# Modulation weights in pieces of 256 rows by 2048 columns, the first shift and scale rows turned on TensorE: a two-layer backbone step on one Trainium2 core

## The reference

```python
def modulation(cond, w, b):                      # w: (1024, 6144)
    m = jnp.einsum('bd,de->be', jax.nn.silu(cond), w) + b
    return [t[:, None, :] for t in jnp.split(m, N_MOD, axis=-1)]   # 6 rows of 1024

shift1, scale1, gate1, shift2, scale2, gate2 = mods
h = rms_norm(x, lw['norm1']) * (1 + scale1) + shift1
z = jnp.einsum('bsd,de->bse', h, lw['w_in'])     # projections q, kv, qr, kr, vr, ...
...                                              # attention, retention, gated MLP
x = x + gate1 * jnp.einsum('bsd,de->bse', mix, lw['w_out'])
h2 = (rms_norm(x, lw['norm2']) * (1 + scale2) + shift2)
...                                              # router, 16 experts
x = x + gate2 * y
```

## Time and profile before

| | |
|---|---|
| median of three runs | 2380.5 us |
| the profiled execution | 2377.39 us, span 2375.6 us |
| PE busy | 2141.1 us, 90% of the span |
| DVE busy | 1230.3 us, 52% |
| ACT busy | 818.0 us, 34% |
| Pool busy | 266.3 us, 11% |
| mean of granted TensorE clock | 0.948 of full speed |
| moved by DMA | 417.13 MB, mean 176 GB/s |

### The profile page before, as it was taken

The page is one execution under the profiler, slowest core; times in us unless marked ns, Lnnn a source line. Parts: engine busy times, 40 slices in busy tenths (PEclk is TensorE's granted clock), DMA queues, the critical chain, the costliest instruction groups (busy, mean ns, idle before and its releaser), DMA issues.

```text
span 2375.6 us, 25634 instructions
## 1 busy us (share of the span) xinstructions
PE 2141.1 (90%) x10487; PEld 1604.0 (68%) x10487; DVE 1230.3 (52%) x1630; ACT 818.0 (34%) x1030; POOL 266.3 (11%) x222
## 2 busy tenths in 40 slices
PE   1899989999999969999849999999999996799992
PEld 0587555488886448888627855647888844688881
DVE  0386455322222448888655844532232234788883
ACT  1123533100000127887532155221000011587881
POOL 2133020100000021000031411001000000110002
PEclk9899989999999959999969999999999996799996
DMA  7226440221134269999551337011121133699984
GB/s 264 107 71 226 149 151 1 74 87 71 36 107 160 99 235 370 415 409 412 212 217 36 109 116 240 10 71 54 62 81 72 40 146 142 226 414 415 411 356 151
DMA packets 113912, 417.13 MB, mean 176 GB/s; under 512 B 7801, under 2 KB 9961, under 8 KB 89089
## 3 DMA queue, kind: packets, MB, share of 16 engines
q1 hardware_dynamic: 89088, 329.27, 36.5%
q0 software_dynamic: 19920, 68.31, 7.6%
q10 hardware_dynamic: 4784, 17.87, 1.8%
HBM read 378.89 MB, written 36.54 MB: 175 GB/s over the span
## 4 chain that ended last, share of the span: by engine, by line
PE 88%; DVE 5%; DMA 3%; ACT 1%; issue 1%; SPq 0%; PEldq 0%; POOL 0%; DVEq 0%; ACTq 0%; POOLq 0%
PE ps L655 76%; PE ps L773 3%; PE ps L785 2%; PE ps L666 2%; PE ps L1039 1%; DMA ring_lo<-in_w_mod_dram 1%; PE ps L1050 1%; DMA work<-y_dram,slots_u 1%; DVE work L1627 1%; PE ps L774 1%; DVE work L1902 1%; DVE work L1904 1%; DVE work L1905 1%; SPq L448 0%; DMA work<-h_dram,slots_u 0%
## 5 line engine op out<-in xcount | busy, mean ns | idle before, releaser
L1859 DVE TENSOR_TENSOR expert_low<-ring_lo,expert_high 128x2048 fp32r<-128x2048 f32 x172 | 386.2, 2285 | 2.9 <-ACT expert_high L1392 2.9
L1392 ACT ACTIVATE expert_high<-ring_lo 128x2048 fp32r<-128x2048 f32 x172 | 326.3, 1914 | 108.0 <-PE ps L655 88.4
L655 PE MATMUL ps<-ring_lo,hT 128*128 128x512 f32 (+1 forms) x800 | 315.8, 552 | 12.5 <-ACT hT L1206 12.3
L655 PEld LDWEIGHTS ps<-ring_lo,hT 128*128 128x128 f32 x800 | 150.3, 191 | 160.3 <-issue 156.6
L655 PE MATMUL ps<-expert_high,x_high 128*128 128x512 f32 x512 | 207.6, 405 | 9.6 <-DVE expert_low L1859 9.6
L655 PE MATMUL ps<-branch,ring_lo 128*128 128x320 f32 x768 | 214.4, 432 | 0.0
L655 PE MATMUL ps<-expert_high,x_low 128*128 128x512 f32 x512 | 202.2, 395 | 0.0
L1341 ACT ACTIVATE work<-ps 128x640 f32<-128x640 f32 x48 | 33.8, 704 | 485.5 <-PE ps L655 485.4
L655 PE MATMUL ps<-expert_low,x_high 128*128 128x512 f32 x512 | 200.9, 392 | 0.0
L655 PE MATMUL ps<-h_hi,w_hi 128*128 128x320 f32 x768 | 186.2, 324 | 2.6 <-issue 2.6
L655 PEld LDWEIGHTS ps<-branch,ring_lo 128*128 128x128 f32 x768 | 143.5, 190 | 53.3
(11 more groups left out here) (272 smaller groups left out, 3283.4 us busy)
## 6 DMA issues: line engine op xcount, KB each, us to landing
ring_lo<-in_w_up_dram SPq DMA_DIRECT2D x64, 1024.0 KB, 7.9
ring_lo<-in_w_gate_dram SPq DMA_DIRECT2D x54, 1024.0 KB, 7.6
ring_lo<-in_w_down_dram SPq DMA_DIRECT2D x54, 1024.0 KB, 8.1
ring_lo<-in_w_in_dram SPq DMA_DIRECT2D x26, 2048.0 KB, 8.3
ring_lo<-in_w_mod_dram SPq DMA_DIRECT2D x24, 2048.0 KB, 13.6
y_dram<-branch ACTq DMA_DIRECT2D x32, 512.0 KB, 8.3
work<-in_w_down_dram SPq DMA_DIRECT2D x10, 1024.0 KB, 7.9
work<-in_w_gate_dram SPq DMA_DIRECT2D x10, 1024.0 KB, 8.4
```

The source lines that it names most:

```text
L655: return pe.matmul(out, lhsT, rhs, start=(k == 0), stop=(k == n - 1))
L1392: A(e_high[n % HIGH], e_raw[n % RAW], ACT.Copy).then_inc(ec_a.sem, 1)
L1859: TT(out=e_low[n % RAW], in0=e_raw[n % RAW], in1=e_high[n % HIGH].bitcast(F32), op=ALU.subtract).then_inc(el_v.sem, 1)
```

## The change

- **Pieces.** A piece of a group is now 256 rows by all 2048 columns of the group (runs of 8 KB in DRAM), two blocks k. `mod_group` waits for piece k // 2 only when it comes to it.
- **Their own signal.** The last matmul of each piece signals a new semaphore, `mod_pc`; SP waits on that for the piece's slot.
- **Turned on PE.** The rows of group 0, copied by ACT to partitions 32j and 32j+1 of a 128 x 512 area that Pool has set to zero, are transposed whole, with four PE transposes into PSUM bank 6, and DVE picks the 32 columns with one strided copy. Norm1's 8 rows are transposed by themselves and copied with a second DVE instruction. The four stores and two loads of group 0 through `mod_dram` and the waits for them are gone, in both layers.
- **Inputs in two parts.** norm1 and w_spatial (`first_inputs`) are loaded first; the other 12 DMAs (`layer_inputs`) are issued, in layer 0, once piece 2 has landed. PE's wait for them is now after the projections q and kv.

```diff
     def last_read(key):
         if key[0] == "mod":
-            return mod_mm, NGRP * key[1] + key[2] // 4 + 1
+            return mod_pc, MODT * key[1] + key[2] + 1
...
     def source(key):
         if key[0] == "mod":
-            return rows(I["w_mod"][key[1], :, key[2] * 512:(key[2] + 1) * 512]), KD, 512
+            g, j = divmod(key[2], 4)
+            return rows(I["w_mod"][key[1], 2 * P * j:2 * P * (j + 1), 2048 * g:2048 * (g + 1)]), 2, 2048
...
     def mod_group(l, g, b):
         pe.wait_ge(bias_in[g], 16 * (l + 1))
-        for j in range(4):
-            key = ("mod", l, 4 * g + j)
-            pe.wait_ge(full[slot_of[key]], full_at(key))
         for k in range(KD):
+            key = ("mod", l, 4 * g + k // 2)
+            if k % 2 == 0:
+                pe.wait_ge(full[slot_of[key]], full_at(key))
+            wt = slot[slot_of[key]]
             for j in range(4):
-                wt = slot[slot_of["mod", l, 4 * g + j]]
-                pe.matmul(ps[32 * j:32 * j + 2, b, :], scT[:, k:16:KD], wt[:, k * 512:(k + 1) * 512],
-                          start=(k == 0), stop=False)
+                c = 2048 * (k % 2) + 512 * j
+                i = pe.matmul(ps[32 * j:32 * j + 2, b, :], scT[:, k:16:KD], wt[:, c:c + 512],
+                              start=(k == 0), stop=False)
+            if k % 2 == 1:
+                i.then_inc(mod_pc, 1)
...
         pe.wait_ge(mod_ev, MODT * l + 4)
-        w(pe, aux_in, l, aux_in.per)
-        w(pe, modr_in, l, 32)
-        pe.transpose(ps[:, 4, 0:40], mod_rows, ident[0:40, 0:40]).then_inc(au_p.sem, 1)
+        w(pe, au_in, l, 32)
+        pe.transpose(ps[:, 4, 0:KD], norm_rows, ident[0:KD, 0:KD])
+        for c in range(4):
+            i = pe.transpose(ps[:, 6, c * P:(c + 1) * P], mod_area(l, 0)[1][:, c * P:(c + 1) * P], ident)
+        i.then_inc(au_p.sem, 1)
...
+        w(pe, aux_in, l, aux_in.per)
         for s, name in enumerate(("qr", "kr")):
...
     # ACT, start of a layer
-        act.wait_ge(mod_st, 64 * (NGRP * l + 1))
         modulate(0)
...
     # DVE, start of a layer
-        V.tensor_copy(modc, bank(4, 40)).then_inc(mc_v.sem, 1)
+        step.mark(V.tensor_copy(modc[:, 32:40], bank(4, KD)))
+        V.tensor_copy(modc[:, 0:32].rearrange("p (s j c) -> p s j c", s=2, j=4),
+                      bank(6).rearrange("p (c j r) -> p r j c", c=4, j=4)[:, 0:2]).then_inc(mc_v.sem, 1)
+        step.settle()
...
     # Pool, start of the program
+    G.memset(mod_area(0, 0)[1], 0.0).then_inc(zeroed, 1)
+    G.wait_ge(zeroed, 1)
     load_bias(0, 0)
...
+    first_inputs(0)
+    G.wait_ge(full[slot_of["mod", 0, 2]], full_at(("mod", 0, 2)))
     layer_inputs(0)
-    store_mods(0, 0)
-    G.wait_ge(mod_st, 64)
-    first_mod_rows(0)
...
     # Pool, end of layer 0
+    G.memset(mod_area(l + 1, 0)[1], 0.0).then_inc(zeroed, 1)
+    G.wait_ge(zeroed, l + 3)
     load_bias(l + 1, 0)
     w(G, lo_p, l, 1)
+    first_inputs(l + 1)
     layer_inputs(l + 1)
...
     fetch_rows(0)
-    store_mods(l + 1, 0)
-    G.wait_ge(mod_st, 64 * (NGRP * (l + 1) + 1))
-    first_mod_rows(l + 1)
```

More of the change, by code:

```diff
@@ L223, in trunk @@
         ws_raw = aux[:, 768:1280]
-        mod_rows = aux[0:40, 1280:1408]
+        norm_rows = aux[0:8, 1280:1408]
         kc_raw = aux[:, 1408:1536]
@@ L234, in trunk @@
         mod_mm = sem("mod_mm")
+        mod_pc = sem("mod_piece_read")
         mod_ev = sem("mod_ev")
@@ L278, in trunk @@
         full = [sem(f"slot{s}_full") for s in range(6)]
-        aux_in = signal("aux_in", 16 * 14)
-        modr_in = signal("mod_rows_in", 32)
+        au_in = signal("norm_and_spatial_in", 32)
+        aux_in = signal("aux_in", 16 * 12)
         xs_out = signal("xs_out", 16)
@@ L1933, in spread, with first_inputs @@
                 return G.dma_start(out, ap.partition_broadcast(P))
+            def first_inputs(l):
+                G.dma_start(norm_rows, I["norm1"][l].rearrange("(k p) -> k p", p=P)).then_inc(au_in.sem, 16)
+                G.dma_start(ws_raw.rearrange("p (g j) -> p g j", g=4),
+                            I["w_spatial"][l].rearrange("g i j -> i g j")).then_inc(au_in.sem, 16)
             def layer_inputs(l):
-                G.dma_start(mod_rows[32:40, :], I["norm1"][l].rearrange("(k p) -> k p", p=P)).then_inc(aux_in.sem, 16)
                 for out, nm in ((qk_gain[:, 0:DH], "q_norm"), (qk_gain[:, DH:2 * DH], "k_norm"),
@@ L1941, in layer_inputs @@
                     spread(out, I[nm][l]).then_inc(aux_in.sem, 16)
-                G.dma_start(ws_raw.rearrange("p (g j) -> p g j", g=4),
-                            I["w_spatial"][l].rearrange("g i j -> i g j")).then_inc(aux_in.sem, 16)
                 with nc.allow_non_contiguous_dma(reason="512 numbers, once per layer"):
@@ L2004, in _ @@
                     G.memset(zeros, 0.0).then_inc(zeroed, 1)
-                    G.wait_ge(zeroed, 1)
+                    G.wait_ge(zeroed, 2)
                     for half in range(2):
@@ L2035, in _ @@
                 w(G, xs_out, l, 16)
-                G.wait_ge(mod_st, 64 * NGRP * (l + 1))
+                G.wait_ge(mod_st, 128 * (l + 1))
                 w(G, cm_v, l, NT)
@@ L2077, in _ @@
                 fetch_rows(0)
-                if l + 1 < LAYERS:
-                    store_mods(l + 1, 0)
-                    G.wait_ge(mod_st, 64 * (NGRP * (l + 1) + 1))
-                    first_mod_rows(l + 1)
                 for e in range(1, NE):
```

## The result

The changed kernel takes 2361.7 us in the median of five runs (2359.9 to 2368.0), the kernel before, timed beside it, 2379.2 (2376.4 to 2380.7): a ratio of 0.9936, with a 95% interval of 0.9918 to 0.9954. It is 15.2 us faster by that ratio. The profiled execution took 2361.74 us around a span of 2359.9, against 2377.39 and 2375.6 before, 15.7 less. The forecast was 24.0 less. The time lies inside the range, by its upper end.

A forecast was written before the change was run, and what follows sets the result against it. TensorE bounds nearly the whole span, standing still at the start for modulation weights and rows. Terms -23.5 - 1.0 + 0.2 + 0.3 = -24.0 us took 2377.4 to 2353.4; forecast 2354 us, range 2347 to 2362.

The forecast's parts named there:

- forecast 35.0: Start of layer 0: the last piece of group 0's modulation weights lands at 35.0 us, where before it was 42.9.
- forecast 3.4 and 2.5: Start: after its landing piece 3's 16 matmuls take 3.4 us at the lower clock, ACT's copy of the rows 2.5.
- the step on q's weights: First projection: q's weights follow piece 3 and land at 45.5 to 48.5 us, in time for 48.8; no PE wait.
- I take even shares: DMA engines at the start: two busy queues were taken to share evenly, judged from bytes moved; called the weak point.
- rival B: First projection: q's weights come late behind inputs and x store; projection at 53 us, total 2358 us; chance 0.08.
- the forecast start: The first projection starts at 48.8 us instead of 72.27, 23.5 us earlier.
- rival A: Last piece held up by inputs, or 8 KB runs bring nothing: landing 40.2 to 42.9, total 2359 to 2362 us; chance 0.14.
- three signs of being wrong: Last piece landing after 40 us, PE waiting for q's weights, or later stages giving time back.
- the forecast's later terms: After the start: -1.0 us at layer 0's gather of h, +0.2 for four waits, +0.3 at layer 1's start.
- The 2.0: Start: held-back inputs, about 0.6 MB in flight beside piece 3, delay its landing by 2 us.
- The 33: Start: without the held-back inputs the last piece would land at 33 us, 32.0 at 425 GB/s.
- rival C: SP's queue takes more with 8 KB packets: pieces by 30.5, x at 31.5, projection at 48.6 us; chance 0.09.

The follow-up runs named there:

- e3: Changed kernel, but both the 12 layer inputs and the store of x are issued only once q's weights have landed; median 2354.6 us, ratio 0.9901.
- e1: Changed kernel, but the store of x is issued only once q's weights have landed; median 2356.0 us, ratio 0.9908.
- e2: Changed kernel, but the 12 layer inputs wait for q's weights while the store of x goes early; one run, 2358.3 us.
- e5: Changed kernel, but group 0's shift and scale rows go through DRAM again in both layers; median 2365.2 us, ratio 0.9941.
- e11: e3 plus ten unread filler matmuls, 1, 2 and 5 behind pieces 0, 1 and 2, two during ACT's row copy; median 2349.9 us, ratio 0.9878.
- e12: e11 with three filler matmuls behind piece 2 instead of five; median 2349.7 us, ratio 0.9878.
- e4: Changed kernel, but the store of x goes in four transfers of 256 columns, with runs of 1 KB; one run, 2362.0 us.
- e6: Changed kernel, but the 12 layer inputs are issued at the start as before, not after piece 2; median 2360.2 us, ratio 0.9922.
- e10: Changed kernel, but x is loaded in eight transfers of 256 columns, with runs of 1 KB; one run, 2365.8 us.
- e8: The changed kernel again, unaltered, as common measure beside e5 to e7; median 2361.4 us, ratio 0.9931.
- e7: Changed kernel, but with the old pieces of 512 columns (runs of 2 KB) and the group's signal; median 2370.1 us, ratio 0.9962.
- e9: Changed kernel, but SP waits for the group's last matmul, not each piece's own, before reloading the slots; median 2369.7 us, ratio 0.9962.

## Why the prediction was right in part

**Right: the place and most of the road.** PE stood still at the start for weights and rows, the change took both waits away, and from the second projection to the last expert's matmuls the lead grew by no more than 0.5 us. Piece 3 came at 34.3 (forecast 35.0), its burst cost 3.4 and the rows' copy 2.4 (forecast 3.4 and 2.5). In e3, where nothing stands in q's way, the bias took 1.9 as forecast, and from the first transpose to the projection it is 5.6 (forecast 6.0): the projection starts at 47.8. That its span is 24.1 us shorter, against 24.0 forecast, is in part luck: 24.5 at the start, 2.0 more on the way, 2.4 lost at the end.

**Wrong: the step on q's weights, which put PE's wait for them at nothing.** It said "At half the bandwidth q lands at about 45.5; at a third, at 48.5. Needed: 48.8." They landed at 51.8, and PE waited 6.3 us. Two things in it failed. The first is the rate. From piece 3's landing at 34.3 until then the engines moved some 6.0 MB, of which q was 2.1, a third, as allowed for (254, then 383, 411 and 400 GB/s); but 2.1 MB at a third in the 13.5 us from 35.0 means 470 GB/s, which no row of before reached, while 35 to 40 us ran at 254 GB/s with the small ones. At the 400 GB/s that its half was reckoned with, a third lands at 50.7, already 1.9 us late. The second is "I take even shares". Even was the number of packets, not of bytes: q's are half as large as the store's, so it had a third. The trace of before had this to show. From 10 to 15 us x's queue moved 1.37 MB and the weights' 0.65; piece 0 and x came out about even because piece 0 had started first. The same holds of the weights of "qr" and the store of x, where they ran side by side (from 70 to 72 us 136 packets against 129, 0.28 MB against 0.53).

This was rival B, given 0.08, and e1 to e3 show it: take either companion away and the wait is gone. The cost against the forecast start is 3.1 us. The time measured is also the price of rival A, 2359 to 2362, but not by its road: piece 3 was not late. That the time lies in the range is thus no merit of the sum. Of the three signs of being wrong that the prediction named, two came: PE waits for q's weights, and the end gives time back.

**Not priced: what the wait does to the clock.** Rival B gave 2358 for a start at 53. The wait itself also left PE at 1.2 GHz for about the first 6 us of the projection: 13.53 us instead of 10.56, another 3.0. The Trainium skill, "TensorE: Matmul & The Clock Gate", section "HAM oscillation — how this bites in real kernels", warns of waits for transfers between bursts of matmuls. It was weighed for the modulation bursts, where it is hidden; it bit behind them, at the one burst that is on the chain. Without the wait the projection took 10.56 in all of e1, e2, e3, e5, e11 and e12; with a wait of 4.5 to 7.5 us it took 12.2 to 13.5 in e4, e6 to e10 and the changed kernel. So the price is 1.6 to 3.0 us; of the same kernel e8 paid 1.6.

**Sum.** 24.0 less 15.7 is 8.3 us: 3.1 for q, 3.0 for the clock, 2.2 later. Between the second projection (17.4 us ahead) and the last expert's matmuls (17.8) the changed kernel gains 0.4 or 0.5, as much as the forecast's later terms (1.0 less 0.5) come to, though not in the waits: that for the first rows of h is no shorter. The 2.2 are at the very end, from the last expert's matmuls to the end of the span (15.7). The prediction had no term there. The chain there has a row of PE's sequencer at the branch behind the last expert, which the chain of before passes by another engine:

```profile
2315.65 4.10 PEldq L1158
```

e8 has the same row, and e3 loses 2.4 us there (26.5 us ahead at the last expert's matmuls, 24.1 at the end). By e5 the row goes with the turn on PE, and 1.5 of the 2.2 us with it. Why the branch then takes 4.1 us instead of 0.4, and where the other 0.7 go, was not tried.

**Right by another road: piece 3.** The 35.0 was made of 33 and 2.0 for the inputs beside it. The 2.0 is refuted: piece 3 comes at 34.3 with the inputs beside it (e6), behind piece 2 (changed), or behind q (e3). The 33 was then 1.3 too low, and the two errors nearly cancel, which is luck. And x was to stay at 19 to 20; it came at 28.5. That is rival C's mechanism, stopped short of its price: ACT's squares and roots were done at 37.0 (38.78 less 1.80 of idle time), before its copies were wanted. e7 shows that the runs of SP's queue cause it, and the packets show how. The Trainium skill, "DMA: Bandwidth & Descriptors", section "Queues, rings and completion order", has the engines take a packet of each queue in turn. The traces agree with it: 331 packets against 335, 180 against 182, 341 against 342. e4 and e10 are no test of it, since Pool's packets stayed at about 4 KB. What larger runs in q's load would give, or a store in packets that really are smaller, was not tried.

**The parts.** Against the changed kernel's 2361.4 to 2361.7: without the turn on PE +3.8 and without the deferral about -1 (neither a difference that can be told by the medians), without the pieces and their signal +8.7, without the signal alone +8.3, of which its profile shows 2.3 at the start. In e7, likewise, the end of the first projection is 4.2 us later (69.7 against 65.5), so half of its 8.7 lies behind that; in its profile 4 us of it are a stretch at the lower clock at 205 us. The parts don't add up, since all hang on one wait for q.

## What to carry to other kernels

A transfer that is released earlier lands earlier only if little else is on the engines: q's weights, sent out 36 us earlier, landed 10 us earlier. Count the bytes of every queue from its release to its need, with shares by the size of each queue's packets as the profile has them and at a rate that a stretch with such a mixture has shown, and put behind it whatever is needed later. Look whether an edit that is to change packets did change them. And price a wait of PE with the clock after it: here 6.3 us of waiting cost 3.0 more (1.6 in e8), and a few matmuls of no use, put where PE would stand idle, gave back 4.3 us at the start.

## What the runs showed of the hardware

Two busy queues moved nearly the same number of packets in the same time, whatever the packets' size, so the bytes went by size. Longer runs in SP's queue therefore push Pool's back: x landed at 19.6 us beside runs of 2 KB and at 28.5 beside runs of 8 KB. A load can also wait before its first packet: in e9 SP's queue moved none from 39 to 43 us, though q was issued at 39.57, and Pool's moved 413.

Runs of 1 KB in place of 4 KB in a DMA of Pool did not make its packets smaller: in e4 they held 3.7 KB on average from 45 to 50 us.

Beside the small inputs a 2.1 MB transfer took 13.4 us, alone 5.5: the 1.64 MB of inputs cost it 8 us, and the 2.6 MB of the store 6.

The granted clock falls to about 0.5 in the middle of attention too, with PE busy throughout, in some profiles and at differing places. All profiles have it low somewhere around 300 us; these stretches come on top. The changed kernel's stretch at 290 us:

```profile
290.00:295.00 5.00, 4.15 (x40) 3.12 (x39) 2.95 (x9) 2.78 (x9) 0.00 (x0) 1.00 1.05 387
```

The stretch before and the same one in e5's profile (2376.9 us, the longest of its runs):

```profile
285.00:290.00 5.00, 5.00 (x34) 1.80 (x27) 1.05 (x3) 2.25 (x4) 1.24 (x3) 0.99 1.05 399
290.00:295.00 5.00, 5.00 (x29) 3.59 (x27) 1.85 (x4) 1.75 (x5) 1.00 (x2) 0.50 1.06 387
```

By these rows it isn't idleness that brings it down: PE is busy 5.00 of 5 us before the clock falls. (That it is also busy 5.00 behind it says less, since the same work takes longer at the lower clock.) Such stretches were seen in e2, e5, e7, e9, e10 and e11. Their stages lost 3 to 7 us on the kernel before: 4 in e2 and e7, 6 and 6.5 in e5, 7 in e9, 6 in e10, 3 in e11. They are the likeliest source of the 5 to 10 us between runs of one kernel here. What sets them off was not found.
